# Two RMS norms ahead of matrix products, with the rows turned by a product with a diagonal of reciprocals

## The chip, the core and the metric

The kernel runs on one core of a Trainium2 chip. The core has the engines that the profile names PE (matrix products), DVE, ACT, POOL (GpSimd) and SP, which here issues the DMA transfers. The metric is the device time of one execution in microseconds, the median of several runs. Lower is better.

## The reference

A first block (attention and causal pooling, then a gated feed-forward stage with a short convolution) is followed by a second block (a state-space mixer and an mLSTM mixer side by side, then a mixture of experts). There are 256 tokens of width 1024, all in fp32. Around the change it computes:

```python
x = x + mix                                   # attention's output product
h = rmsnorm(x, norm_ffn_g)                    # first norm of this text ("ffn")
u = causal_dwconv(h @ w_up, conv_w, conv_b)
gate, val = split(u)
x = x + (silu(gate) * val) @ w_down
x = rmsnorm(x, norm_final_g)                  # end of the first block
h = rmsnorm_2(x, norm1_w)                     # second norm of this text ("n1")
p = h @ w_in_2                                # second block's input product
# rmsnorm(x, g) = x * rsqrt(mean(x*x) + EPS) * g
```

Two norms follow each other between the blocks. The kernel applies both at once. With y = x * norm_final_g, h is y * norm1_w over the root of mean(y*y) + EPS*mean(x*x) + EPS*EPS, one reciprocal per row.

## The kernel before, in words

The 256 tokens are two row tiles of 128 (t = 0, 1). X holds the residual rows, H is a scratch of the same shape. The weights come in pieces of 1 MB through a ring of five `raw` buffers. To keep fp32 accuracy, each piece is split in two fp32r parts: ACT copies it to WH (`split`, L544), DVE writes the rest raw - WH to WL (L1077). Activations are split likewise: HTH and HTL hold the transposed normed rows (feature blocks of 128 on the partitions), MXH and MXL the inputs of output and down products. `three` (L2022 to L2025) issues the three products that make one. There are three such ring slots of WH and WL. SP's queue fetches a piece when its ring buffer has been split.

Each engine runs a list written out by hand, in order, with semaphores between the engines; nothing is scheduled at run time. PE's list sets the order of the work.

The stretches of this text:

- Output product of the attention, `wo`: for t, for half c, products into bank 4 + 2c + t. Each finished bank releases DVE's `add_to_x` (L1114), which adds it into X.
- First norm. ACT squares rows of X with a row sum (`squares`, L551): all of tile 0, tile 1 in two halves. DVE makes mean + EPS (L1080, L1119), POOL raises it to -0.5 (`power`, L1973). DVE and for half of tile 1 ACT scale the rows into H (`rows` L1091, `row1` L556). PE turns H by transposes, two feature blocks per bank of 6, 7, 4, 5 (`norm_columns`, L2064). ACT writes HTH, scaled by the norm's weight (`columns`, L566), and DVE HTL (L1100). PE waits for two column blocks at a time (`col_ready`).
- `warm(n, w)` (L2029) issues n products of the identity with itself. Their result is not used. They stand in the list where PE would wait.
- Feed-forward: 11 groups g of 256 features. `feature_tiles` makes gate and value features (bank 4, 5 or 6, 7), DVE and ACT do the convolution, the silu and the split to MXH, MXL. The down product of group g - 1 follows group g's, all four quarters (t, half) into banks 0 to 3, each group's 24 products of 512 columns.
- Last group: `last_down` does tile 0 first, then tile 1's two halves.
- Second norm. DVE adds into X and writes X*g to H (`weighted_rows`, L1321). ACT squares both X and H. DVE joins the sums (L1334, L1342, L1119), scales H by the reciprocal (L1091), ACT does half of tile 1 (L556), then PE, ACT and DVE turn it as above. The first piece of the second block (`xbc`) follows.

## Time and profile before

| | us |
|---|---|
| median of three runs | 1025.98 (1025.85 to 1026.82) |
| the profiled execution | 1027.49 |
| its span, first to last instruction | 1025.70 |
| mean granted clock of PE | 0.997 |
| PE busy | 1006.3 |
| DVE busy | 840.8 |
| ACT busy | 704.4 |

The page gives each engine's busy time, and the chain of work that ended last, followed back from the end. A timeline lists one engine's instructions by start. A matmul's duration is longer than its step, since matmuls overlap: the distance from one start to the next is what it costs. An fp32 product counts as two MATMUL instructions ("x2"), an fp32 transpose as one. In brackets stands how long the engine had stood idle before and what released it.

### The profile page before, as it was taken

To read this page: it belongs to the slowest core of one execution; us is meant where nothing else is said; L and a number is where in the kernel's file an instruction comes from. 1 tells how busy PE (TensorE), PEld (TensorE's weight loads), DVE (VectorE), ACT (ScalarE), POOL (GpSimd) and SP (SyncE) were. 2 spreads that over 40 slices of the span, in tenths; PEclk is the share of its full clock that TensorE was granted. 3 is DMA by queue.
4 is the path that set the end of the run, shared out by engine and by line. 5 is a ranking of instruction groups with operands and counts; after the bars stand their busy time and mean duration, and the time that the engine had idled before them with its cause. 6 is when DMAs were issued, how large, how long until landed. Compare 5 with 4: busy or idle time off the path is not lost.

```text
span 1025.7 us, 14943 instructions
## 1 busy us (share of the span) xinstructions
PE 1006.3 (98%) x5588; PEld 869.2 (85%) x5588; DVE 840.8 (82%) x1038; ACT 704.4 (69%) x856; POOL 40.7 (4%) x44
## 2 busy tenths in 40 slices
PE   7999999999999999999999999999999999999997
PEld 6788999999989888999888888888888888888884
DVE  5855876666677887797859899999999999999987
ACT  5664655555565755576445788888888888888874
POOL 2001000000000020100220100000000000000000
PEclk9999999999999999999999999999999999999999
DMA  9734456474725455343216999999999999999971
GB/s 342 282 123 144 155 174 222 147 226 147 228 72 197 164 165 158 126 140 118 83 34 222 349 362 368 363 378 368 374 360 378 359 376 368 376 355 383 364 294 44
DMA packets 82709, 253.60 MB, mean 247 GB/s; under 512 B 4160, under 2 KB 42176, under 8 KB 62656
## 3 DMA queue, kind: packets, MB, share of 16 engines
q1 hardware_dynamic: 82624, 252.51, 68.2%
q8 instruction: 48, 0.79, 0.3%
q14 instruction: 37, 0.30, 0.1%
HBM read 251.44 MB, written 1.05 MB: 246 GB/s over the span
## 4 chain that ended last, share of the span: by engine, by line
PE 83%; DVE 7%; ACT 3%; issue 3%; POOL 0%; POOLq 0%; DVEq 0%; ACTq 0%
PE bank L2023 25%; PE bank L2025 25%; PE bank L2024 24%; DVE WL L1077 2%; ACT WH L544 2%; PE bank L2525 1%; PE bank L2565 1%; DVE CV L1369 1%; PE bank L2029 1%; PE bank L2484 0%; PE bank L2493 0%; PE bank L2597 0%; PE bank L2050 0%; PE bank L2458 0%; PE bank L2129 0%
## 5 line engine op out<-in xcount | busy, mean ns | idle before, releaser
L1077 DVE TENSOR_TENSOR WL<-raw,WH 128x2048 fp32r<-128x2048 f32 x230 | 524.6, 2303 | 89.6 <-ACT WH L544 86.0
L544 ACT ACTIVATE WH<-raw 128x2048 fp32r<-128x2048 f32 x231 | 440.6, 1914 | 82.2 <-PE bank L2025 72.2
L2023 PE MATMUL bank<-WH,MXH 128*128 128x512 f32 x552 | 218.4, 396 | 0.6 <-DVE WL L1077 0.6
L2025 PE MATMUL bank<-WH,MXL 128*128 128x512 f32 x552 | 215.2, 390 | 0.0
L2024 PE MATMUL bank<-WL,MXH 128*128 128x512 f32 x552 | 215.0, 390 | 0.0
L2023 PE MATMUL bank<-HTH,WH 128*128 128x256 f32 x576 | 165.0, 286 | 1.2 <-DVE HTL L1100 1.2
L2025 PE MATMUL bank<-HTH,WL 128*128 128x256 f32 x576 | 162.9, 283 | 0.0
L2024 PE MATMUL bank<-HTL,WH 128*128 128x256 f32 x576 | 162.9, 283 | 0.0
L2023 PE MATMUL bank<-WH,HTH 128*128 128x512 f32 x400 | 159.5, 399 | 2.3 <-DVE WL L1124 1.9
L2024 PE MATMUL bank<-WL,HTH 128*128 128x512 f32 x400 | 155.9, 390 | 0.0
L2023 PEld LDWEIGHTS bank<-WH,MXH 128*128 128x128 f32 x552 | 103.6, 188 | 29.3 <-issue 8.4
L2025 PEld LDWEIGHTS bank<-WH,MXL 128*128 128x128 f32 x552 | 103.6, 188 | 22.2
L2024 PEld LDWEIGHTS bank<-WL,MXH 128*128 128x128 f32 x552 | 103.7, 188 | 20.3
L2023 PEld LDWEIGHTS bank<-HTH,WH 128*128 128x128 f32 x576 | 110.4, 192 | 2.1 <-issue 1.5
L2024 PEld LDWEIGHTS bank<-HTL,WH 128*128 128x128 f32 x576 | 110.5, 192 | 0.5
L2025 PEld LDWEIGHTS bank<-HTH,WL 128*128 128x128 f32 x576 | 110.4, 192 | 0.0
L2023 PEld LDWEIGHTS bank<-WH,HTH 128*128 128x128 f32 x400 | 75.5, 189 | 17.8 <-issue 2.1
L2024 PEld LDWEIGHTS bank<-WL,HTH 128*128 128x128 f32 x400 | 75.3, 188 | 14.4
L2025 PE MATMUL bank<-WH,HTH 128*128 128x512 f32 x208 | 81.4, 392 | 0.0
L2025 PE MATMUL bank<-WH,HTL 128*128 128x512 f32 x200 | 78.1, 391 | 0.0
L1973 POOL TENSOR_TENSOR sm<-sm,cn 128x1 f32<-128x1 f32 (+3 forms) x18 | 17.1, 957 | 856.1 <-DVE sm L1080 509.2
L1369 DVE SCALAR_TENSOR_TENSOR CV<-bank,pt,CV 128x255 f32<-128x255 f32 (+2 forms) x84 | 40.3, 481 | 9.0 <-ACT CV L733 6.8
(411 smaller groups left out, 1063.3 us busy)
## 6 DMA issues: line engine op xcount, KB each, us to landing
raw<-in_exp_w_up SPq DMA_DIRECT2D x52, 1024.0 KB, 7.2
raw<-in_exp_w_gate SPq DMA_DIRECT2D x52, 1024.0 KB, 7.2
raw<-in_exp_w_down SPq DMA_DIRECT2D x52, 1024.0 KB, 7.4
raw<-in_w_in SPq DMA_DIRECT2D x34, 1024.0 KB, 5.2
raw<-in_w_up SPq DMA_DIRECT2D x22, 1024.0 KB, 5.3
raw<-in_w_down SPq DMA_DIRECT2D x11, 1024.0 KB, 5.2
raw<-in_w_out SPq DMA_DIRECT2D x8, 1024.0 KB, 5.1
raw<-in_w_o SPq DMA_DIRECT2D x4, 1024.0 KB, 5.4
```

The lines of the kernel that those rows point to most:

```text
L544: e.activation(WH[i % HL][:, :], raw[i % RAW][:, :], ACT.Copy).then_inc(a_wh, 1)
L1077: e.tensor_tensor(l, r, h.bitcast(F32), ALU.subtract).then_inc(v_wl, 1)
L1369: m = e.scalar_tensor_tensor(out=u[:, sh:256], in0=b[:, 0:256 - sh], scalar=ptcol(cw, n * tap + j), in1=u[:, sh:256], op0=ALU.mult, op1=AL ...
L1973: e.tensor_tensor(v, v, const("mh", v.shape[1]), ALU.pow).then_inc(g_rstd, 1)
L2023: e.matmul(out_, ah, bh, start=start, stop=False, skip_group_check=skip)
L2024: e.matmul(out_, ah, bl, start=False, stop=False, skip_group_check=skip)
L2025: return e.matmul(out_, al, bh, start=False, stop=stop, skip_group_check=skip)
L2029: e.matmul(bank[w][:, 0:128], ident, ident, start=True, stop=True)
L2525: m = e.transpose(bank[TBK][:, k * 128:(k + 1) * 128], SG[u % 2][:, k:512:4], ident)
L2565: m = e.matmul(bank[GU[0][0]][:, :], XST[kh][:, k, 0:128], raw[i % RAW][:, k * 512:(k + 1) * 512], start=(kh == 0 and k == 0), stop=(kh == ...
```

## The change

- At both norms, H is no longer written. DVE multiplies the identity by the row's reciprocals, a 128x128 diagonal (`diagonal`, into the scratch TMP), and PE multiplies X's feature blocks as stationary tile with it. That turns and scales in one. These are plain fp32 products where transposes were.
- Each feature block gets its own bank (`NORM_BANKS`), with a semaphore count for each block on PE, ACT and DVE (`bank_columns`), where there were two to a bank.
- The final norm's weight is no longer multiplied into the rows. DVE folds it into the next norm's column weight (128x8), ACT squares the weight once in the third feed-forward group (`gb2`), and the weighted square sum is a DVE instruction (`weighted_sum`) over ACT's squares of X times `gb2`.
- The last two groups' down products change order. Filler products become fewer at both places. One small weight gets another buffer.

What DVE has in its list at the second norm, from tile 0's adds on: each row is an instruction with its output, inputs and shape; x2 are two of them. Before:

```order
L1114 TENSOR_TENSOR X<-bank,X 128x512 x2
L1321 TENSOR_TENSOR H<-X,BIG 128x1024
L1114 TENSOR_TENSOR X<-bank,X 128x512
L1321 TENSOR_TENSOR H<-X,BIG 128x512
L1334 TENSOR_SCALAR sm<-sm 128x1
L1119 SCALAR_TENSOR_TENSOR sm<-sm 128x1
L1114 TENSOR_TENSOR X<-bank,X 128x512
L1321 TENSOR_TENSOR H<-X,BIG 128x512
L1342 TENSOR_SCALAR sm<-sm 128x1
L1119 SCALAR_TENSOR_TENSOR sm<-sm 128x1
L1091 TENSOR_SCALAR H<-H,sm 128x1024
L1119 SCALAR_TENSOR_TENSOR sm<-sm 128x1 x2
```

Now, from the same adds on. ISA is the weighted sum with its read-out:

```order
L1123 TENSOR_TENSOR X<-bank,X 128x512 x2
L1333 ISA CV,sm<-CV,BIG 128x512
L1333 ISA sm 128x1
L1333 ISA CV,sm<-CV,BIG,sm 128x512
L1333 ISA sm 128x1
L1123 TENSOR_TENSOR X<-bank,X 128x512
L1338 SCALAR_TENSOR_TENSOR sm<-sm 128x1
L1355 SCALAR_TENSOR_TENSOR sm<-sm 128x1
L1333 ISA CV,sm<-CV,BIG 128x512
L1333 ISA sm 128x1
L1338 SCALAR_TENSOR_TENSOR sm<-sm 128x1
L1123 TENSOR_TENSOR X<-bank,X 128x512
```

The rows X*g and their scaling (H) are gone; the last add comes behind three of the four weighted sums.

PE's list at the end of the last down product, before:

```order
L2025 MATMUL bank<-WH,MXL 128x512
L2023 MATMUL bank<-WH,MXH 128x512
L2024 MATMUL bank<-WL,MXH 128x512
L2025 MATMUL bank<-WH,MXL 128x512
L2029 MATMUL bank<-cn 128x128 x21
L2064 MATMUL bank<-cn,H 128x128 x8
L2029 MATMUL bank<-cn 128x128 x3
L2064 MATMUL bank<-cn,H 128x128 x8
L2029 MATMUL bank<-cn 128x128 x3
L2023 MATMUL bank<-HTH,WH 128x256
```

And now, where cn is the identity and TMP the diagonal:

```order
L2042 MATMUL bank<-WH,MXL 128x512
L2040 MATMUL bank<-WH,MXH 128x512
L2041 MATMUL bank<-WL,MXH 128x512
L2042 MATMUL bank<-WH,MXL 128x512
L2046 MATMUL bank<-cn 128x128 x3
L2078 MATMUL bank<-TMP,X 128x128 x8
L2046 MATMUL bank<-cn 128x128 x4
L2078 MATMUL bank<-TMP,X 128x128 x8
L2040 MATMUL bank<-HTH,WH 128x256
```

The filler of 21 products ahead of the turns is 3 now, and the turns have become products with the diagonal.

The diff, cut to its core:

```diff
+PARTS = [(0, 0, 512), (0, 512, 1024), (1, 0, 512), (1, 512, 1024)]
+NORM_BANKS = {"ffn": (6, 4, 5, 0, 1, 2, 3, 7), "n1": (6, 4, 5, 0, 1, 2, 7, 3)}
...
+        gb, gb2 = big(9216, D), big(10240, D)
+        diag = [TMP[:, t, 0:128] for t in range(T)]
-        ws_raw = big(10240, 256)
+        ws_raw = big(0, 256)
...
+                for k, w in enumerate(NORM_BANKS[name]):
+                    e.wait_ge(p_cols, COL[name, k])
+                    e.activation(dh[:, k, :], bank[w][:, 0:256], ACT.Copy, scale=ptcol(gname, k)).then_inc(a_colh, 1)
...
-            row1("ffn", X)
-            columns("ffn", "norm_ffn_g", 0, (6, 7, 4, 5), HTH)
...
+            bank_columns("ffn", "norm_ffn_g", HTH)
...
+                if g == 2:
+                    e.wait_ge(d_gb, 16)
+                    e.activation(gb2, gb, ACT.Square).then_inc(a_gb2, 1)
...
-            e.wait_ge(v_xadd, 6)
-            squares("n1", 0, X[:, 0, :], ss[:, 0:1])
-            e.wait_ge(v_fx, 1)
-            squares("n1", 1, H[:, 0, :], part[0])
-            for c in range(2):
-                cs = slice(c * 512, (c + 1) * 512)
-                e.wait_ge(v_xadd, 7 + c)
-                squares("n1", 2 + 2 * c, X[:, 1, cs], part[1 + 2 * c])
-                e.wait_ge(v_fx, 2 + c)
-                squares("n1", 3 + 2 * c, H[:, 1, cs], part[2 + 2 * c])
-            row1("n1", H)
-            columns("n1", "norm1_w_2", 0, (6, 7, 4, 5), HTH)
+            for i, (t, c0, c1) in enumerate(PARTS):
+                e.wait_ge(v_xadd, XADD["n1", i])
+                if t:
+                    e.wait_ge(v_gsum, 1 if c0 == 0 else 2)
+                e.activation(cvf[:, c0:c1], X[:, t, c0:c1], ACT.Square, accum_out=part[i]).then_inc(a_sq, 1)
+            bank_columns("n1", "norm_final_g", HTH)
...
+            def diagonal(name, t):
                 e.wait_ge(g_rstd, RSTD[name, t])
-                e.tensor_scalar(H[:, t, 0:n], src[:, t, 0:n], rs[:, t:t + 1], None, ALU.mult).then_inc(v_h0, 1)
+                e.tensor_scalar(diag[t], ident, rs[:, t:t + 1], None, ALU.mult).then_inc(v_diag, 1)
...
             mean_eps(rs[:, 0:1], ss[:, 0:1], D).then_inc(v_ms, 1)
-            e.wait_ge(a_sq, SQ["ffn", 1])
-            mean_eps(part[1], ss[:, 1:2], D).then_inc(own.up(), 1)
+            e.wait_ge(a_sq, SQ["ffn", 2])
+            mean_eps(part[4], part[0], D).then_inc(own.up(), 1)
+            diagonal("ffn", 0)
             e.wait_ge(p_used, PI["wo", 1, 1] + 1)
-            add_to_x(1, 1, 7)
-            rows("ffn", 0, X)
-            e.wait_ge(a_sq, SQ["ffn", 2])
-            chained(rs[:, 1:2], part[0], 1.0 / D, part[1]).then_inc(v_ms, 1)
-            rows("ffn", 1, X)
-            columns("ffn", "norm_ffn_g", 0, (6, 7, 4, 5), HTH, HTL)
+            add_to_x(3, 7)
+            e.wait_ge(a_sq, SQ["ffn", 3])
+            chained(rs[:, 1:2], part[1], 1.0 / D, part[4]).then_inc(v_ms, 1)
+            diagonal("ffn", 1)
+            bank_columns("ffn", "norm_ffn_g", HTH, HTL)
...
-            def weighted_rows(t, c0, c1):
-                e.tensor_tensor(H[:, t, c0:c1], X[:, t, c0:c1], gb[:, c0:c1], ALU.mult).then_inc(v_fx, 1)
+            def weighted_sum(i, start):
+                t, c0, c1 = PARTS[i]
+                e.wait_ge(a_sq, SQ["n1", i])
+                e.wait_ge(own.sem, own.n)
+                return e.tensor_tensor_reduce(cvf[:, c0:c1], cvf[:, c0:c1], gb2[:, c0:c1], 1.0 / D, start, ALU.mult, ALU.add,
+                                              wsum[:, i:i + 1])
+            def eps_of(i, start):
+                e.wait_ge(own.sem, own.n)
+                e.scalar_tensor_tensor(out=esum[:, i:i + 1], in0=part[i], scalar=EPS / D, in1=start, op0=ALU.mult,
+                                       op1=ALU.add).then_inc(own.up(), 1)
+            ng = ptcol("norm_final_g", 0, 8)
+            e.tensor_tensor(ng, ng, ptcol("norm1_w_2", 0, 8), ALU.mult).then_inc(own.up(), 1)
             e.wait_ge(p_tok0, TOK0["fin0"])
-            add_to_x(0, 0, 0)
-            add_to_x(0, 1, 1)
-            e.wait_ge(d_gb, 16)
-            e.wait_ge(v_xadd, 6)
-            weighted_rows(0, 0, D)
+            add_to_x(0, 0)
+            add_to_x(1, 1)
+            e.wait_ge(a_gb2, 1)
+            weighted_sum(0, EPS * EPS).then_inc(v_gsum, 1)
+            e.wait_ge(v_gsum, 1)
+            weighted_sum(1, wsum[:, 0:1]).then_inc(v_gsum, 1)
             e.wait_ge(p_tok0, TOK0["fin1"])
-            add_to_x(1, 0, 2)
-            e.wait_ge(v_xadd, 7)
-            weighted_rows(1, 0, 512)
-            e.wait_ge(a_sq, SQ["n1", 0])
-            e.tensor_scalar(part[5], ss[:, 0:1], EPS / D, EPS * EPS, ALU.mult, ALU.add).then_inc(own.up(), 1)
-            e.wait_ge(a_sq, SQ["n1", 1])
-            chained(rs[:, 0:1], part[0], 1.0 / D, part[5]).then_inc(v_ms, 1)
+            add_to_x(2, 2)
+            e.wait_ge(v_gsum, 2)
+            eps_of(0, wsum[:, 1:2])
+            e.wait_ge(own.sem, own.n)
+            e.scalar_tensor_tensor(out=rs[:, 0:1], in0=part[1], scalar=EPS / D, in1=esum[:, 0:1], op0=ALU.mult,
+                                   op1=ALU.add).then_inc(v_ms, 1)
+            weighted_sum(2, EPS * EPS).then_inc(own.up(), 1)
+            eps_of(2, wsum[:, 2:3])
             e.wait_ge(p_used, PI["down", NG - 1] + 1)
-            add_to_x(1, 1, 3)
-            e.wait_ge(v_xadd, 8)
-            weighted_rows(1, 512, D)
-            e.wait_ge(a_sq, SQ["n1", 2])
-            e.tensor_scalar(part[6], part[1], EPS / D, EPS * EPS, ALU.mult, ALU.add).then_inc(own.up(), 1)
-            e.wait_ge(a_sq, SQ["n1", 3])
-            chained(part[7], part[2], 1.0 / D, part[6]).then_inc(own.up(), 1)
-            rows("n1", 0, H)
-            e.wait_ge(a_sq, SQ["n1", 4])
-            chained(part[6], part[3], EPS / D, part[7]).then_inc(own.up(), 1)
-            e.wait_ge(a_sq, SQ["n1", 5])
-            chained(rs[:, 1:2], part[4], 1.0 / D, part[6]).then_inc(v_ms, 1)
-            rows("n1", 1, H)
-            columns("n1", "norm1_w_2", 0, (6, 7, 4, 5), HTH, HTL)
+            add_to_x(3, 3)
+            diagonal("n1", 0)
+            weighted_sum(3, esum[:, 2:3]).then_inc(own.up(), 1)
+            e.wait_ge(own.sem, own.n)
+            e.scalar_tensor_tensor(out=rs[:, 1:2], in0=part[3], scalar=EPS / D, in1=wsum[:, 3:4], op0=ALU.mult,
+                                   op1=ALU.add).then_inc(v_ms, 1)
+            diagonal("n1", 1)
+            bank_columns("n1", "norm_final_g", HTH, HTL)
...
+            def norm_columns(name, t):
+                e.wait_ge(v_diag, DIAG[name, t])
+                for k, w in enumerate(NORM_BANKS[name]):
+                    if t == 0 and name == "ffn" and k == 7:
+                        e.wait_ge(v_xadd, XADD["ffn", 3])
+                    m = e.matmul(bank[w][:, t * 128:(t + 1) * 128], X[:, t, k * 128:(k + 1) * 128], diag[t], start=True,
+                                 stop=True)
                     if t:
                         m.then_inc(p_cols, 1)
...
-                if cols and k % 2 == 0:
+                if cols in NORM_BANKS:
+                    e.wait_ge(v_coll, COL[cols, k])
+                elif cols and k % 2 == 0:
                     e.wait_ge(v_coll, COL[cols, k // 2])
...
-            warm(5, 0)
-            norm_columns("ffn", 0, (6, 7, 4, 5))
-            warm(2, 0)
-            norm_columns("ffn", 1, (6, 7, 4, 5))
-            warm(3, 0)
...
+            wo_half(0, 0, 0, 512).then_inc(p_tok0, 1)
+            wo_half(0, 1, 0, 512).then_inc(p_tok0, 1)
+            wo_half(1, 0, 0, 512).then_inc(p_used, 1)
+            wo_half(1, 1, 0, 512).then_inc(p_used, 1)
+            norm_columns("ffn", 0)
+            warm(1, 0, 256)
+            norm_columns("ffn", 1)
...
+            def last_down(g, f, t, c0, n):
+                j, s = 2 * g + f, 2 * (g % 2) + f
+                wh, wl = last_w[g - NG + 2]
+                ts, hf, cs = slice(t * 128, (t + 1) * 128), c0 // 512, slice(c0, c0 + n)
+                return three(bank[2 * t + hf][:, c0 % 512:c0 % 512 + n], MXH[:, s, ts], MXL[:, s, ts], wh[:, f, cs],
+                             wl[:, f, cs], False, j == FF - 1)
+            last_w.append(piece(PI["down", NG - 2], 2))
+            e.wait_ge(v_mxl, FF - 2)
+            for c0 in (0, 512):
+                for f in range(2):
+                    last_down(NG - 2, f, 0, c0, 512)
+            for f in range(2):
+                last_down(NG - 2, f, 1, 0, 512)
+            last_w.append(piece(PI["down", NG - 1], 2))
             for f in range(2):
                 e.wait_ge(v_mxl, FF - 1 + f)
-                for hf in range(2):
-                    m = last_down(0, hf, f)
+                for c0 in (0, 512):
+                    m = last_down(NG - 1, f, 0, c0, 512)
             m.then_inc(p_tok0, 1)
-            for hf in range(2):
-                for f in range(2):
-                    m = last_down(1, hf, f)
-                m.then_inc(p_used if hf else p_tok0, 1)
-            warm(21, 7)
-            norm_columns("n1", 0, (6, 7, 4, 5))
-            warm(3, 0)
-            norm_columns("n1", 1, (6, 7, 4, 5))
-            warm(3, 0)
+            for f in range(2):
+                m = last_down(NG - 2, f, 1, 512, 512)
+            m.then_inc(p_used, 1)
+            for f in range(2):
+                m = last_down(NG - 1, f, 1, 0, 512)
+            m.then_inc(p_tok0, 1)
+            for f in range(2):
+                m = last_down(NG - 1, f, 1, 512, 512)
+            m.then_inc(p_used, 1)
+            warm(3, 7)
+            norm_columns("n1", 0)
+            warm(4, 7, 256)
+            norm_columns("n1", 1)
...
```

## Rows read from the trace of the kernel before

**Rows 1.** The page, its chain that ended last, shares of the span by engine.
```profile
PE 83%; DVE 7%; ACT 3%; issue 3%; POOL 0%; POOLq 0%; DVEq 0%; ACTq 0%
```

**Rows 2.** Timeline of PE, first norm: start, duration, line, operation [idle before <-releaser].
```profile
98.41 1.27 PE L2029 MATMUL bank<-cn 128*128 128x128 f32 x10
...
101.46 1.09 PE L2064 MATMUL bank<-cn,H 128*128 128x128 f32 x8
...
103.83 0.35 PE L2023 MATMUL bank<-HTH,WH 128*128 128x256 f32 x1 [0.61 <-DVE HTL L1100]
```

**Rows 3.** Timeline of PE, second norm and the piece behind it.
```profile
290.80 4.85 PE L2029 MATMUL bank<-cn 128*128 128x128 f32 x42
...
297.72 1.09 PE L2064 MATMUL bank<-cn,H 128*128 128x128 f32 x8
...
300.09 0.35 PE L2023 MATMUL bank<-HTH,WH 128*128 128x256 f32 x1 [0.61 <-DVE HTL L1100]
...
306.05 0.28 PE L2023 MATMUL bank<-HTH,WH 128*128 128x256 f32 x1
```

**Rows 4.** Timeline of DVE and ACT over the same stretch.
```profile
98.61 0.69 DVE L1114 TENSOR_TENSOR X<-bank,X 128x512 f32<-128x512 f32 x1 [1.08 <-PE bank L2025]
...
99.34 0.63 ACT L551 ACTIVATE CV<-X 128x512 f32<-128x512 f32 x1 [2.00 <-DVE X L1114]
...
100.09 0.16 DVE L1119 SCALAR_TENSOR_TENSOR sm<-sm 128x1 f32<-128x1 f32 x1
100.92 0.49 DVE L1091 TENSOR_SCALAR H<-X,sm 128x512 f32<-128x512 f32 x1 [0.67 <-POOL sm L1973]
...
101.94 3.02 ACT L566 ACTIVATE HTH<-bank,pt 128x256 fp32r<-128x256 f32 x8 [0.30 <-PE bank L2064]
102.81 3.23 DVE L1100 SCALAR_TENSOR_TENSOR HTL<-bank,pt,HTH 128x256 fp32r<-128x256 f32 x8 [1.40 <-ACT HTH L566]
104.80 3.76 ACT L544 ACTIVATE WH<-raw 128x2048 fp32r<-128x2048 f32 x2
106.80 4.49 DVE L1077 TENSOR_TENSOR WL<-raw,WH 128x2048 fp32r<-128x2048 f32 x2 [0.76 <-ACT WH L544]
```

**Rows 5.** Timeline of PE, the gate piece: second feature tile, next piece.
```profile
106.91 0.28 PE L2023 MATMUL bank<-HTH,WH 128*128 128x256 f32 x1
...
109.79 0.28 PE L2023 MATMUL bank<-HTH,WH 128*128 128x256 f32 x1
```

**Rows 6.** Timeline of PE, attention: plain fp32 products.
```profile
46.79 0.44 PE L2128 MATMUL bank<-BIG,H 128*128 128x128 f32 x2
...
61.31 0.39 PE L2154 MATMUL bank<-BIG 128*128 128x128 f32 x2
61.53 0.39 PE L2155 MATMUL bank<-BIG 128*128 128x128 f32 x2
```

**Rows 7.** Timeline of DVE ahead of the second norm.
```profile
285.26 0.42 DVE L1315 TENSOR_TENSOR MXL<-CV,MXH 128x256 fp32r<-128x256 f32 x1 [0.55 <-ACT MXH L706]
287.06 2.29 DVE L1077 TENSOR_TENSOR WL<-raw,WH 128x2048 fp32r<-128x2048 f32 x1 [1.38 <-ACT WH L544]
289.27 1.28 DVE L1114 TENSOR_TENSOR X<-bank,X 128x512 f32<-128x512 f32 x2
```

**Rows 8.** DVE groups by form: line, operation, count | busy us, mean ns | idle.
```profile
L1829 DVE SCALAR_TENSOR_TENSOR CV<-bank,sm,CV 128x512 f32<-128x512 f32 x26 | 19.4, 747 | 1.0 <-PE bank L2025 1.0
...
L1514 DVE CUSTOM_DVE_ANT_0 BIG<-bank,BIG 128x256 f32<-128x256 f32 x8 | 3.4, 419 | 0.0
```

**Rows 9.** Waits of ACT from 98 to 285: us in total, times, longest.
```profile
ACT WH L544 <- PE bank L2025: 25.4, 10, 2.8
```

**Rows 10.** PE timeline, and a window (us, busy of 5 engines, PEclk, DMA).
```profile
12.54 0.47 PE L2023 MATMUL bank<-WH,HTH 128*128 128x512 f32 x1 [1.90 <-DVE WL L1124]
...
535.47 3.04 PE L2458 MATMUL bank<-BIG 128*128 128x36 f32 x24
...
538.00:541.00 3.00, 3.00 (x15) 3.00 (x15) 2.21 (x16) 0.21 (x1) 0.00 (x0) 0.50 0.00 0
```

More of the change, by code:

```diff
@@ L113 @@
 COL = numbered([(s, j) for s in ("mix", "attn", "ffn", "n1", "ssd0", "ssd1", "ml0", "ml1")
-                for j in range(4 if s in ("mix", "ffn", "n1") else 2)])
+                for j in range({"mix": 4, "ffn": 8, "n1": 8}.get(s, 2))])
 P_CUM = numbered(["sums", "turned", "max"])
@@ L119 @@
                 + ["ssd0", "ssd1", "ml0", "ml1"] + [(s, t) for s in ("n2", "out") for t in range(T)])
-SQ = numbered([("mix", t) for t in range(T)] + [("ffn", i) for i in range(3)] + [("n1", i) for i in range(6)]
+PARTS = [(0, 0, 512), (0, 512, 1024), (1, 0, 512), (1, 512, 1024)]
+XADD = numbered([(n, i) for n in ("ffn", "n1") for i in range(4)] + [("out", i) for i in range(4)])
+SQ = numbered([("mix", t) for t in range(T)] + [("ffn", i) for i in range(1, 4)] + [("n1", i) for i in range(4)]
               + [("n2", c, t) for c in range(2) for t in range(T)] + [("out", i) for i in range(3)])
@@ L1104, in columns, with bank_columns @@
                     m.then_inc(v_coll, 1)
+            def bank_columns(name, gname, dh, dl):
+                for k, w in enumerate(NORM_BANKS[name]):
+                    e.wait_ge(a_colh, COL[name, k])
+                    e.scalar_tensor_tensor(out=dl[:, k, :], in0=bank[w][:, 0:256], scalar=ptcol(gname, k),
+                                           in1=dh[:, k, :].bitcast(F32), op0=ALU.mult,
+                                           op1=ALU.subtract).then_inc(v_coll, 1)
             def evac(name, t, piece):
@@ L1355, in vector @@
[L1355 removed]
+            mean_eps(part[5], part[0], D).then_inc(own.up(), 1)
+            chained(r1[:, 0:1], part[1], 1.0 / D, part[5]).then_inc(v_ms, 1)
+            mean_eps(part[6], part[2], D).then_inc(own.up(), 1)
+            chained(r1[:, 1:2], part[3], 1.0 / D, part[6]).then_inc(v_ms, 1)
             def residual(t):
@@ L2025, in three, with warm @@
                 return e.matmul(out_, al, bh, start=False, stop=stop, skip_group_check=skip)
-            def warm(n, w):
+            def warm(n, w, c=0):
                 for _ in range(n):
-                    e.matmul(bank[w][:, 0:128], ident, ident, start=True, stop=True)
+                    e.matmul(bank[w][:, c:c + 128], ident, ident, start=True, stop=True)
             def piece(i, k):
```

100 lines of the change are left out of this document (40 added, 60 removed).

## The prediction

> **What bounds the kernel now.** I read the page first: the chain that ended last is 83% PE [rows 1]. So a change counts only where PE stands still or does work that is thrown away. The granted clock was full over nearly the whole span. Then I read the timeline of PE at the two norms the diff touches; there the reader should look for the `ident` products of `warm` (L2029), which compute nothing and only fill waits. After the attention's output product PE starts filler at 98.41, turns two row tiles, and starts the first useful product at 103.83 [rows 2]. That is 5.42 us. After the last down product filler starts at 290.80 and useful work at 300.09, 9.29 us [rows 3]. Together 14.7 us, 1.4% of the time, is all that the two norms can give. Third, the timelines of DVE and ACT over the same stretches, for what sets these starts.
>
> At the first norm it is a chain on tile 1: last add to X at 98.61, square at 99.34, scalar step at 100.09, the power on GpSimd, row scaling at 100.92 (0.49 us for half a row), PE's turn at 101.46, ACT's HTH columns at 101.94, DVE's HTL columns at 102.81 and PE at 103.83 [rows 2, 4]. From then on PE takes a column block whenever DVE has it. The gate's second feature tile starts at 106.91, the next piece at 109.79 [rows 5].
>
> **First norm, what changes.** Everything up to 100.92 stays: same adds, squares and power. Then:
> - DVE scales a 128x128 diagonal instead of 512 columns. The 512 took 0.49 us and a one-column step 0.16 [rows 4]; I take 0.24. PE starts at 101.21 instead of 101.46 (bounds 101.13 and 101.46).
> - PE makes plain products, two passes each, instead of one-pass turns. The nearest rows are fp32 products 128x128 with a new stationary tile each time: pairs start 0.22 us apart at 61.31 and 61.53, and the two passes take 0.39. After a switch of kind, at 46.79, they took 0.44 [rows 6]. I take 0.224 per product, at worst 0.28. Eight take 1.8 us, so PE has tile 1 done at 103.0. Tile 0's eight lie in the time that filler had.
> - ACT starts after the first product rather than after two turns. The delay is the same two passes, 0.48 us (101.46 to 101.94 [rows 2, 4]), so ACT starts at 101.69.
> - DVE waited for two ACT columns and now waits for one. Eight ACT columns take 3.02, eight of DVE 3.23 [rows 4]: a step is 0.37 on ACT and 0.39 on DVE. So DVE starts 0.5 after ACT, at 102.19 rather than 102.81. It ends at 105.42 instead of 106.04.
> - PE may take each block as it is ready, not each pair. After the last block 3 products are left instead of 6, 0.36 us less. PE's own work ends at the same point (103.0 plus 24 products of 0.12, from the 2.88 us between 106.91 and 109.79). The second feature tile starts at about 105.95, 0.96 earlier.
> - What is late next is the split of the following weight piece. ACT starts it 2.86 us after its first column (104.80 after 101.94), so at 104.55 and DVE's half at 106.55 rather than 106.80; it takes 2.29, so PE can start at about 109.0. PE itself would be there at 108.83. Gain: 109.79 less 108.98, **0.81 us**. Bounds: 0.3 with products of 0.28 and the diagonal at 0.49; 1.0 if the split is no limit.
>
> **Last down product and second norm.** The order of the products changes so that tile 0 is done after 30 of 48 rather than 24. Two effects. PE now comes to the last MXL block at about 285.33, and that block is only ready at 285.68 (285.26 plus 0.42 [rows 7]), so PE waits half a microsecond and ends at 291.3 instead of 290.8. This costs nothing as long as DVE is the later one: DVE is in a split until 289.35 (287.06 plus 2.29), and its adds start at 289.27 in the kernel before [rows 7]. For the same reason the earlier tile 0 earns nothing. If that cover went, the price is 0.5.
>
> DVE's chain decides. New are four weighted sums of squares, one behind each add's square. The nearest row is the same custom instruction on 256 elements, 0.42 us (one source in PSUM); scaled by its neighbours I take 0.70 for 512. Upper bound 0.83: the 512 three-source form at 0.75 [rows 8] plus a read-out. Lower bound 0.6, the step between two 512 adds [rows 7]. Gone are the product rows X*g and their squares on ACT. With 0.69 per add and 0.75 from a square's start to the step that reads it (99.34 to 100.09 [rows 4]):
> - adds at 289.33 and 289.93, first weighted sum 290.8 to 291.5, second to 292.3;
> - add of tile 1's first half 292.2, its square until 293.7, third weighted sum to 294.4, last add at 294.58;
> - tile 0's diagonal ends at 295.43, PE starts its products at 295.5 (tile 0 has slack);
> - from the last add to the second diagonal: the first norm took 2.31 us from add to scaling (98.61 to 100.92 [rows 4]), plus 0.78 for the fourth weighted sum and its wait. That is 297.67; PE starts tile 1 at 297.97. Before it was 297.72 [rows 3].
>
> So the start is 0.25 **later**, and the finer hand-over gives it back. PE's eight products end at 299.76, then 24 products: second feature tile at 302.7, where it now is 303.17 (306.05 less 2.88). ACT's columns start at 298.45, the split of the next piece 2.86 later as above, at 301.31 (now 297.72 + 0.48 + 2.86 = 301.06), and PE can start that piece at 305.74 rather than 306.05. Gain: **0.31 us**. Bounds: a loss of 0.5 (weighted sums 4 x 0.13 dearer, products at 0.28) and a gain of 1.2 (the waits in front of the four sums, about 0.9 in my list, vanish).
>
> **Edits priced at nothing.** The 1024-element square of the weight on ACT in the third FFN group, about 1.1 us: ACT waits for PE ten times there, 25.4 us in all [rows 9]. If it hit PE it would cost its 1.1. The 128x8 product of two weights is one short DVE step. The wider weight table and the moved buffer for the small projection's weights change no order on the DMA queue. Two more one-column steps behind the split are beside PE's work.
>
> **Sum.** 0.81 + 0.31 = 1.12 us. The profiled execution took 1027.49 (span 1025.70, 1.79 outside it) and would take 1026.37. The median of the timed runs is 1.51 lower, 1025.98; the sum carried over is 1024.86. A shift at these places moves all that follows: PE is the chain's engine up to the end, and the experts' weights are fetched only after the routing, which shifts too.
>
> **Rivals.**
> - *The clock drops in the wait (slower).* PE had 42 passes of filler, 4.85 us, ahead of the second norm [rows 3]; now it has 3 products, ends them at 292.0 and idles until 295.5. Before, this trace has one dip of the granted clock: in the routing, from 538 to 541, it was 0.50, the level of 1.2 GHz [rows 10], and what came ahead were products of only 36 columns. Against it: near 12.5 PE had stood still for 1.9 us [rows 10], and the products behind that came at full pace. Nothing here is as long as 3.5. If it drops, 3.0 us at 0.50 cost 1.5 us of work, its two edges a little more; I take 1.7. Then 1024.86 + 1.7 = 1026.6, slower than before. It decides from the point where half-rate work reaches tile 1's products; a second dip in a row gives 1028.3.
>  The Trainium skill, "TensorE: Matmul & The Clock Gate", section "HAM oscillation — how this bites in real kernels", says that long idle gaps between bursts return PE to half rate and that each restart is then paid cold; by it this rival would be the rule and the time 1026.6. The same page, "Part 4: PE-mode transpose", says that transposes don't count as busy for that gate; by it the new plain products would help to hold the clock and the forecast would stand. No row here separates the two.
> - *The weighted sums and the two-pass products are dearer.* Both at their upper bounds: 0.3 at the first norm, minus 0.4 at the second. 1026.0; half way it is 1025.5. For it: four of them lie in line on one engine. Against: each row of a similar form sits near my value.
> - *More comes back.* The waits ahead of the sums vanish and the split is no limit: 1.0 + 1.2 gives 1023.8. Against it: each sum needs a square that can start only after the add before it.
> - *The gain is taken back later*, by DVE or by weight transfers in the experts' stage: 1026.0.
>
> **How the numbers follow.** Forecast 0.50 (own range 1024.2 to 1025.7); clock 0.22, of which 0.06 with two dips; dearer steps 0.13; more comes back 0.11; taken back 0.04. 0.2% is 2.05 us, about what a measurement of this kernel can tell from no change, so the bounds are 1023.93 and 1028.03. Faster: most of the fourth case and a little of the forecast's tail, 0.15. Slower: two dips and a little of one, 0.09. The rest, 0.76, is within. The range leaves out the far end of "more comes back" and two dips: 1023.6 to 1027.2.
>
> **What would show it.** First norm: the first HTH-by-WH product about 4.6 us after the last output product instead of 5.4, products 0.22 apart, and the next piece 10.6 us after it instead of 11.4. Second norm: PE idle for about 3.5 us, tile 1's first product 3.4 us after the last add's start, the granted clock at 1.00. The forecast is wrong if the clock row for that stretch shows 0.5, if PE waits for MXL and DVE is no longer the later one, or if a weighted sum takes over 0.85 us.

## The result: a little slower, and why the profiled runs hide it

| | before | after |
|---|---|---|
| median, runs | 1027.15 us, 17 | 1028.24 us, 17 |
| ratio after to before, 95% | | 1.0016 [1.0009, 1.0024] |
| profiled execution, span | 1027.49, 1025.7 | 1027.69, 1025.8 |

The forecast was 1.1 us faster; measured is about 1.6 us slower (0.0016 x 1026; the means of the 17 runs differ by 1.6 too, their medians by 1.1). That is within 0.2%, but outside the range given: carried over to the 1025.98 that the forecast starts from, it is 1027.6, and the range ended at 1027.2. The two profiled spans are equal by chance. The kernel before had a fall of the clock in its routing [rows 10], and after had none there, which is 0.9 us. The remaining 0.7 us come in the experts' stage: at 600 us after is 0.75 us behind, at the last product 0.1. That stage scatters from one trace to the next (e15, described below, goes from 1.1 us ahead to 0.5 behind in it). So I compare starts of the same PE instruction in both traces, ahead of these stages, and not spans.

At the first norm, PE's timeline after (start, duration, line) answers to [rows 2, 5]:

```profile
98.47 1.95 PE L2078 MATMUL bank<-TMP,X 128*128 128x128 f32 x16
...
101.32 2.05 PE L2078 MATMUL bank<-TMP,X 128*128 128x128 f32 x16 [0.68 <-DVE TMP L1092]
103.13 0.36 PE L2040 MATMUL bank<-HTH,WH 128*128 128x256 f32 x1
...
109.06 0.39 PE L2040 MATMUL bank<-HTH,WH 128*128 128x256 f32 x1
```

The x16 are eight products of two passes each. From the end of the output products (98.47 after, 98.41 before) to the next piece it is 10.59 us (109.06 less 98.47); before it was 11.38 (109.79 less 98.41). The gain is 0.79.

At the second norm, it answers to [rows 3]:

```profile
290.69 0.83 PE L2046 MATMUL bank<-cn 128*128 128x128 f32 x6
294.94 3.68 PE L2078 MATMUL bank<-TMP,X 128*128 128x128 f32 x16 [3.42 <-DVE TMP L1092]
298.44 1.07 PE L2046 MATMUL bank<-cn 128*128 128x128 f32 x8
299.35 1.95 PE L2078 MATMUL bank<-TMP,X 128*128 128x128 f32 x16
301.06 0.36 PE L2040 MATMUL bank<-HTH,WH 128*128 128x256 f32 x1
```

Same stretch, windows (us, busy time of PE, PEld, DVE, ACT, POOL, then the granted clock, as in [rows 10]):

```profile
292.00:294.00 2.00, 0.00 (x0) 0.00 (x0) 1.40 (x6) 0.72 (x2) 0.54 (x1) 1.00 0.90 306
294.00:295.00 1.00, 0.06 (x1) 0.06 (x1) 0.88 (x3) 0.28 (x1) 0.00 (x0) 1.00 0.00 0
295.00:298.00 3.00, 3.00 (x14) 3.00 (x15) 1.21 (x4) 0.45 (x2) 0.55 (x1) 0.51 0.00 0
298.00:299.00 1.00, 1.00 (x9) 1.00 (x8) 0.00 (x0) 0.00 (x0) 0.00 (x0) 0.77 0.00 0
299.00:302.00 3.00, 3.00 (x29) 3.00 (x28) 1.72 (x5) 2.23 (x7) 0.00 (x0) 1.00 0.00 0
```

PE stood still for 3.42 us; then the granted clock fell to 0.5, the 1.2 GHz level. Tile 0's products took 3.68 us where the first norm's took 1.95. Tile 1's could not start before 299.35, though its diagonal was written by 297.38, as DVE's timeline shows:

```profile
294.00 0.68 DVE L1123 TENSOR_TENSOR X<-bank,X 128x512 f32<-128x512 f32 x1
294.60 0.28 DVE L1092 TENSOR_SCALAR TMP<-cn,sm 128x128 f32<-128x128 f32 x1
295.48 0.75 DVE L1333 CUSTOM_DVE_ANT_0 CV<-CV,BIG,sm 128x512 f32<-128x512 f32 x1 [0.59 <-ACT CV L722]
...
297.09 0.29 DVE L1092 TENSOR_SCALAR TMP<-cn,sm 128x128 f32<-128x128 f32 x1 [0.66 <-POOL sm L1990]
```

A second loss lies 38 us further on. At the small projection's turn (`small_turn`, the transpose of a narrow tile) PE waits for ACT's copy of a bank. First the two rows of the kernel before, of a stretch the prediction did not look at (ACT, then PE), then PE's of after. ACT, before:

```profile
337.25 0.36 ACT L778 ACTIVATE TMP<-bank 32x256 f32<-32x256 f32 x1
```

PE, before:

```profile
337.66 0.31 PE L2279 MATMUL bank<-cn,TMP 32*128 32x32 f32 x2
```

PE, after:

```profile
339.44 0.31 PE L2312 MATMUL bank<-cn,TMP 32*128 32x32 f32 x2 [0.68 <-ACT TMP L780]
```

Before, ACT's copy ended at 337.61 (337.25 + 0.36) and PE took it at 337.66, without a wait: two chains arrived together, and either could have been the later. After, PE waits. What comes ahead of ACT's copy is VectorE's convolution, whose first taps are, before and after:

```profile
305.61 1.50 DVE L1369 SCALAR_TENSOR_TENSOR CV<-bank,pt,CV 128x255 f32<-128x255 f32 x3
```

```profile
307.39 1.50 DVE L1386 SCALAR_TENSOR_TENSOR CV<-bank,pt,CV 128x255 f32<-128x255 f32 x3
```

In both kernels ACT's copy starts 31.64 us behind the first tap (337.25 and 339.03). The taps are 1.78 us later in after, and so is the turn.

### The profile page after: what moved, and what is told of

It reads as the page before. It is cut to its first block, busy times and chain, and to the rows that moved or that the text cites. A ratio compares the mean times of both kernels' runs of the same rounds, so it can differ in the third digit from the quotient of the medians.

```text
span 1025.8 us, 14887 instructions
## 1 busy us (share of the span) xinstructions
PE 1003.7 (98%) x5562; PEld 867.6 (85%) x5562; DVE 839.5 (82%) x1043; ACT 701.9 (68%) x851; POOL 40.8 (4%) x44
## 4 chain that ended last, share of the span: by engine, by line
PE 81%; DVE 9%; ACT 5%; issue 2%; POOL 0%; POOLq 0%; DVEq 0%; ACTq 0%
PE bank L2040 24%; PE bank L2042 24%; PE bank L2041 24%; DVE WL L1079 4%; ACT WH L549 3%; DVE CV L1386 1%; PE bank L2558 1%; PE bank L2598 1%; PE bank L2078 1%; PE bank L2517 0%; PE bank L2526 0%; PE bank L2067 0%; PE bank L2145 0%; PE bank L2491 0%; PE bank L2630 0%
```

## The experiments

All twelve were timed in five rounds beside the kernel before. The table has the ratio to the kernel before, what it is in us (of 1026), and how much later than before the same PE instruction starts in the profiled execution, at four points, named by their time in the trace of before. The first useful product is the first HTH-by-WH product behind the second norm; "next piece" is, as in the prediction, the product that begins with the following piece of weights. From each I took off the shift at 12.54 us, which is start-up noise (-0.16 to 0.90 us).

| kernel | ratio [95%] | us | 109.79 next piece | 300.09 first useful product | 337.66 small turn | 471.51 |
|---|---|---|---|---|---|---|
| after | 1.0016 [1.0009, 1.0024] | +1.6 | -0.71 | +0.99 | +1.80 | +1.68 |
| e1_fill18 | 1.0005 [0.9996, 1.0015] | +0.5 | -0.72 | -0.67 | +0.15 | +0.03 |
| e3_fill_turns | 1.0002 [0.9993, 1.0011] | +0.2 | -0.71 | -0.65 | +0.15 | +0.03 |
| e4_before_fill3 | 1.0012 [1.0003, 1.0021] | +1.2 | 0.00 | +0.81 | +0.82 | +0.83 |
| e5_first_norm | 0.9992 [0.9983, 1.0001] | -0.8 | -0.79 | -0.91 | -0.90 | -0.91 |
| e6_old_order | 1.0006 [0.9997, 1.0015] | +0.6 | -0.73 | -0.67 | +0.13 | +0.01 |
| e9_split_early | 0.9989 [0.9980, 0.9998] | -1.1 | -0.73 | -0.67 | -0.79 | -1.15 |
| e10_before_delay | 1.0008 [0.9999, 1.0017] | +0.8 | 0.00 | +0.01 | +0.63 | +0.59 |
| e11_all | 0.9988 [0.9979, 0.9997] | -1.2 | -0.70 | -0.65 | -0.76 | -1.20 |
| e12_both_early | 0.9986 [0.9977, 0.9995] | -1.4 | -0.82 | -0.87 | -0.98 | -1.43 |
| e13_pairs | 1.0003 [0.9995, 1.0012] | +0.3 | +0.11 | +0.90 | +0.90 | +0.45 |
| e14_early_no_fill | 1.0002 [0.9994, 1.0011] | +0.2 | -0.72 | +0.95 | +0.84 | +0.46 |
| e15_first_early | 0.9991 [0.9982, 1.0000] | -0.9 | -0.89 | -1.12 | -1.11 | -1.11 |

The last column and the timed difference agree within 0.6 us in each row, though each interval is about 1 us to either side. So the steps are read from the traces, one for each kernel, and the timings say no more than that their sum lasts to the end. I stop at 471.51 because the routing behind it sometimes has a fall of the clock of its own, and the experts' stage scatters.

Each timed run also has a mean granted clock. Its median is 0.996 to 0.997 in the three kernels that leave PE idle for over 3 us at the second norm (after, e4, e14), and 0.998 or 0.999 in the other ten and in the runs of the kernel before beside them. One fall of 3.4 us to half would lower the mean by 0.0017 (an estimate, 3.4 x 0.5 of 1026). So the fall at the norm is there in most runs, not only in the profiled ones.

**e1_fill18: the wait filled.**

```diff
-            warm(3, 7)
+            warm(18, 7)
             norm_columns("n1", 0)
```

> The changed kernel with 18 filler products in place of 3 ahead of the second norm's first tile; nothing else differs. Clock theory (PE stands idle for 3.4 us there, and the granted clock falls from 1.00 to 0.50 for the next 3 us): PE idle ahead of the tile falls from 3.42 us to under 0.2, the granted clock is 1.00 from 290 to 300, the 16 products of the first tile take 1.95 us as at the first norm and not 3.68, the next piece (the first product after the second norm, at 306.99 in the changed kernel) starts 1.9 us earlier, and the run is 1.6 to 2.0 us below the changed kernel and about 1 below the kernel before. Rival (the new chain of weighted sums and the fp32 products with a diagonal are what costs): the products stay near 3.7 us or the chain's end moves by nothing, and the time is the changed kernel's within 0.3.

PE's timeline:

```profile
291.03 4.18 PE L2046 MATMUL bank<-cn 128*128 128x128 f32 x36
295.25 2.05 PE L2078 MATMUL bank<-TMP,X 128*128 128x128 f32 x16
297.14 1.06 PE L2046 MATMUL bank<-cn 128*128 128x128 f32 x8
298.03 1.95 PE L2078 MATMUL bank<-TMP,X 128*128 128x128 f32 x16
299.74 0.36 PE L2040 MATMUL bank<-HTH,WH 128*128 128x256 f32 x1
```

and its window:

```profile
295.00:298.00 3.00, 2.96 (x26) 2.77 (x26) 1.40 (x5) 0.72 (x2) 0.55 (x1) 1.00 0.00 0
```

The clock held and the products took 2.05 us. The first useful product and the next piece came 1.66 us earlier than in after (0.99 + 0.67 in the table); 1.9 was expected for the next piece. The time fell by about 1.1 us rather than 1.6 to 2.0, and it did not get below the kernel before: the wait of 0.68 us at the small turn stayed. That sent me to the second loss.

**e3_fill_turns: other filler.** As e1, but 3 products and 30 turns:

```diff
             warm(3, 7)
+            for _ in range(30):
+                e.transpose(bank[7][:, 0:128], ident, ident)
             norm_columns("n1", 0)
```

> The changed kernel with 3 filler products and then 30 turns of 128 x 128 with the identity ahead of the second norm's first tile, some 3.3 us of work in the place of the idle 3.4 us. If any work of PE holds the clock: as the kernel with 18 filler products, 1.00 from 290 to 300, 1.6 to 2.0 us below the changed kernel. If turns do not count as work for the clock (the Trainium skill, TensorE: Matmul & The Clock Gate, on PE-mode transposes): 0.50 behind them, products of 3.7 us, and the changed kernel's time within 0.3.

PE's timeline:

```profile
291.56 3.44 PE L2298 MATMUL bank<-cn 128*128 128x128 f32 x30
295.10 2.05 PE L2078 MATMUL bank<-TMP,X 128*128 128x128 f32 x16
```

3.44 us of turns kept the clock as well as products did. The rule of the Trainium skill ("TensorE: Matmul & The Clock Gate", "Part 4: PE-mode transpose") that transposes don't count as busy is not borne out here, for fp32 turns of this shape and over this length. It rests on one trace and on the mean clock of the 11 runs, 0.998 to 0.999.

**e4_before_fill3: the old kernel with the wait left empty.**

```diff
-            warm(21, 7)
+            warm(3, 7)
```

> The kernel before with 3 filler products in place of 21 ahead of its second norm, so that PE idles there for about 4.2 us; nothing else differs. Clock theory: the granted clock falls to 0.50 behind the idle time, the turns and filler of that norm run at half speed, and the time rises by 0.7 to 2.0 us. Rival (idle time alone is harmless, the fall belongs to the new products or their chain): clock 1.00, and the time of the kernel before within 0.3.

PE's timeline, and below it a window with the granted clock:

```profile
296.08 1.35 PE L2064 MATMUL bank<-cn,H 128*128 128x128 f32 x8 [4.29 <-DVE H L1091]
297.22 1.49 PE L2029 MATMUL bank<-cn 128*128 128x128 f32 x6
298.50 1.87 PE L2064 MATMUL bank<-cn,H 128*128 128x128 f32 x8
```

```profile
297.00:300.00 3.00, 3.00 (x16) 3.00 (x16) 0.49 (x1) 1.55 (x4) 0.30 (x1) 0.50 0.00 0
```

The idle time alone brings the fall, with the old chain and the old turns. It costs 0.8 us there and 1.6 in the changed kernel. That fits with half as much work ahead of the first useful product, sixteen one-pass turns against sixteen two-pass products, but no run separates this from the later start of the fall in e4 (0.7 us behind PE's first turn, against 0.1 behind the first product in after). With e1 and the mean clocks this shows the fall and what brings it. It does not show how long the idle time must be: waits of 1.3 to 2.2 us at 12.54 were followed by products at full pace in every trace that has one, waits of 3.38 us and more at the norm by 0.50, and nothing in between was run.

**e5_first_norm.** The kernel before with the change at the first norm alone. The core of the edit, with the same diagonal and bank-by-bank columns as in the change:

```diff
-            norm_columns("ffn", 0, (6, 7, 4, 5))
...
-            norm_columns("ffn", 1, (6, 7, 4, 5))
...
+            bank_norm(0)
+            warm(1, 0, 256)
+            bank_norm(1)
```

> The kernel before with the change at the first norm alone (products with a diagonal, a bank per block of columns); its second norm, last down and final norm are the old ones. If the first norm's gain of 0.79 us seen in the trace lasts to the end: 0.6 to 0.9 us below the kernel before. If it is given back at a later wait (for data or in the routing): within 0.3 of it.

-0.8 timed, -0.79 at the next piece and -0.91 at 471.51. The first norm's gain lasts. (It was 0.69 at 262 us and 0.91 at 300, so 0.22 of it appeared over the old second norm; where it comes from is open.)

**e6_old_order.** e1 with the old order of the last down product (the two whole groups in sequence, in the last one tile 0 then tile 1).

```diff
-            for c0 in (0, 512):
-                for f in range(2):
-                    last_down(NG - 2, f, 0, c0, 512)
...
+            def last_down(t, hf, f):
```

> The kernel with 18 filler products, with the old order of the last down product put back (whole pairs of groups, tile 0 done after 24 of 48 products in place of 30). In the changed kernel the stage enters the last down product 0.63 us earlier than before and leaves it only 0.11 earlier, after a wait of 0.22 us for the last MXL block. Order theory: with the old order the wait goes, the last down product ends 0.4 to 0.55 us earlier (about 290.2 to 290.6), but the diagonals come at most 0.1 earlier, since VectorE's adds, which stand behind a weight split, set them; the time is that of the kernel with 18 filler products within 0.3. Rival (the end of the product sets the norm): the next piece and the time come 0.5 us earlier.

The filler begins at 290.21 rather than 291.03, of which 0.28 is the start-up shift, so the last down product ends 0.54 us earlier. But the diagonals and the first useful product do not move: -0.67 in both. As forecast, the new order costs 0.5 us while VectorE is the later one, and earns nothing.

**e9_split_early: the second chain.** e1 with ScalarE's split of the next piece ahead of its columns:

```diff
+            split(PI["xbc", 0] + 1)
             bank_columns("n1", "norm_final_g", HTH)
-            split(PI["xbc", 0] + 1)
```

> The kernel with 18 filler products, with ScalarE's half of the split of the next weight piece put ahead of its eight columns of the second norm; nothing else differs. With 18 filler products PE starts its first useful product 0.35 us earlier than the kernel before, yet 38 us later, at its small turn (L2312 <- ACT TMP), it waits 0.7 us and is 0.47 us later than before. Theory: from the second norm to that turn the chain of VectorE and ScalarE (split, then taps of the convolution) sets the time, not PE; with ScalarE's split out of the way VectorE's starts 0.8 to 1.1 us earlier, the wait at the small turn falls under 0.1, and the run is 0.7 to 0.8 us below the kernel with 18 filler products. Rival (the wait at the small turn has another source, the small weights' buffer that was moved, say): the wait stays at 0.7 and the time is the same.

PE's row at the small turn, with no wait:

```profile
336.71 0.31 PE L2312 MATMUL bank<-cn,TMP 32*128 32x32 f32 x2
```

DVE, where its split no longer waits for ACT:

```profile
298.49 3.23 DVE L1110 SCALAR_TENSOR_TENSOR HTL<-bank,pt,HTH 128x256 fp32r<-128x256 f32 x8 [1.27 <-ACT HTH L573]
301.63 2.28 DVE L1079 TENSOR_TENSOR WL<-raw,WH 128x2048 fp32r<-128x2048 f32 x1
```

The small turn comes 0.94 us earlier than in e1, and the product at 471.51 by 1.18; timed, 1.6. That is more than the 0.7 to 0.8 expected. The part between the small turn and 471.51 I did not trace. The split costs nothing in its new place: ACT did nothing there in after between 295.45 and 299.77.

**e10_before_delay: the same chain in the old kernel.**

```diff
             split(PI["xbc", 0] + 1)
+            e.tensor_scalar(H[:, 0, :], H[:, 0, :], 1.0, None, ALU.mult).then_inc(own.up(), 1)
             mean_eps(r1[:, 0:1], ss[:, 0:1], D).then_inc(v_ms, 1)
```

> The kernel before with one more VectorE operation of 1024 columns (about 1 us, it rewrites a buffer that is free) between the split behind the second norm and the first taps; nothing else differs. If VectorE's chain sets the time up to the small turn and had almost no slack in the kernel before: PE waits 0.8 to 1.0 us at the small turn (L2279 <- ACT TMP) and the time rises by as much. If PE sets it and VectorE had room: no wait there and the kernel before's time within 0.2.

DVE with the added step, and below it PE at the small turn:

```profile
305.22 0.69 DVE L1353 TENSOR_SCALAR H<-H 128x1024 f32<-128x1024 f32 x1
305.82 0.21 DVE L1080 TENSOR_SCALAR sm<-sm 128x1 f32<-128x1 f32 x2
```

```profile
338.23 0.31 PE L2280 MATMUL bank<-cn,TMP 32*128 32x32 f32 x2 [0.56 <-ACT TMP L778]
```

The step was 0.60 us long (305.22 to 305.82), not 1, and PE waited 0.56 us for it. So the kernel before had 0.04 us of room at this point. A later VectorE was paid here almost in full.

**e11_all.** Filler, old order, early split, and VectorE's four one-column steps behind the convolution:

```diff
                 conv(c, (4, 5) if c % 2 else (6, 7))
 
+            fin_sums()
```

> The changed kernel with all that the traces so far point to mended: 18 filler products, the old order of the last down product, ScalarE's split ahead of its columns, and VectorE's four one-column steps for the final norm (0.54 us) put behind the convolution. Theory: clock at 1.00 at the norm, no wait at the small turn, PE's next piece after the second norm 0.3 to 0.8 us earlier than in the kernel with 18 filler products; time 1.0 to 1.5 us below that kernel and 0.8 to 1.5 below the kernel before. Rival (the gain is handed to another wait behind the small turn): the same as the kernel with the split alone put early.

The same as e9 at every point within 0.05 us: once the split is early, the two other edits give nothing, which is what the rival said. The size expected, 0.8 to 1.5 below the kernel before, was met (1.2), but the next piece came only 0.07 us earlier than in e1, not 0.3 to 0.8.

**e14_early_no_fill.** After with the early split alone.

> The changed kernel with ScalarE's split of the next piece put ahead of its columns and nothing else: 3 filler products as in the changed kernel. It gives the price of the clock alone, with the wait at the small turn out of the way. Theory: PE idle 3.4 us, granted clock 0.50 for about 3.4 us behind it, first tile's products 3.7 us, no wait at the small turn; first useful product and small turn 1.3 to 1.8 us later than with 18 filler products and the early split, time 1.2 to 1.8 us above that kernel's 1025.9 (1027.1 to 1027.7). Rival (the slow clock is hidden behind the waits for VectorE's chain): within 0.4 of 1025.9.

PE's timeline, and below it the window behind the idle time:

```profile
295.83 3.50 PE L2078 MATMUL bank<-TMP,X 128*128 128x128 f32 x16 [3.38 <-DVE TMP L1092]
```

```profile
296.00:299.00 3.00, 3.00 (x16) 3.00 (x17) 1.20 (x4) 2.13 (x3) 0.54 (x1) 0.53 0.00 0
```

The clock's price alone: 1.62 us at the first useful product against e9 (0.95 + 0.67), and 1.61 at 471.51. The timed medians are 1.15 us apart, the ratios 1.3.

**e13_pairs.** e11 with `k | 1` in place of `k` in the three waits of the hand-over.

```diff
-                    e.wait_ge(v_coll, COL[cols, k])
+                    e.wait_ge(v_coll, COL[cols, k | 1])
```

> The kernel with all four mends, but at both norms every block waits for its neighbour too (p_cols, a_colh and v_coll for k | 1), so that blocks go from PE to ScalarE to VectorE to PE in pairs as in the kernel before. If the hand-over block by block is what gives the gain: the first useful product comes 0.6 to 0.9 us later at both norms, the next piece 0.3 to 0.5 later at the first one, and the time is 0.4 to 1.0 above the kernel with all mends. If the split behind the columns sets the next piece in any case: the next piece and the time within 0.2.

Block by block is worth more than I expected: 0.81 us at the first norm's next piece (+0.11 against -0.70) and as much again at the second, 1.65 together at 471.51; timed, 1.5 against 0.4 to 1.0 expected. With pairs nothing is left of the gain at the first norm. PE does not wait for the split at the next piece when columns come in pairs.

**e12_both_early.** e11 with the same move at the first norm (`split(13)` ahead of `bank_columns("ffn", ...)`).

> The kernel with all four mends and, at the first norm too, ScalarE's split of the next piece ahead of its columns. ScalarE stands idle for 1.73 us there before its columns in the changed kernel and the split takes 1.9, so the columns start 0.1 to 0.3 us later, but PE's wait of 0.4 us for the split piece goes. Expected: next piece 0.0 to 0.3 us earlier, time equal to the kernel with all mends within 0.3. Rival (the weight slot comes free late, and ScalarE is held up): columns over 0.5 us later and the time 0.3 or more above.

DVE's timeline there, which answers to its row at 106.80 in [rows 4]:

```profile
105.50 4.48 DVE L1079 TENSOR_TENSOR WL<-raw,WH 128x2048 fp32r<-128x2048 f32 x2
```

ACT's columns still start at 101.85, the next piece comes 0.12 us earlier and the second one behind it too (0.23 at 471.51 against e11). This is the fastest kernel here, 0.9986 [0.9977, 0.9995]; its lead on e9 and e11 is seen in the trace only.

**e15_first_early.** e5 with that move. It tells what the second norm's part is worth once mended.

> The kernel before with the change at the first norm alone and, there, ScalarE's split of the next piece ahead of its columns; second norm, last down and final norm are the old ones. Beside the kernel with all mends at both norms it tells what the second norm's part of the change is worth once it is mended. If that part earns what the traces show (small turn of the fully mended kernel at 336.9 against 337.7 before, of which 0.65 came from the first norm): 0.1 to 0.6 us above the fully mended kernel's 1025.35. If it earns nothing: within 0.1 of it. Both norms: next piece at about 109.0.

At 471.51 it is 0.32 us behind e12; timed 0.9991 against 0.9986, too close to call. So nearly all the good of the change is in its first half. Over the second norm itself the old form is even ahead: e15's first useful product comes 0.25 us before e12's (-1.12 against -0.87) and its next piece 0.14 (-1.12 against -0.98). What e12 has at 471.51 it gains behind the small turn, and that I did not trace. Part of e12's lag is filler that is now too long. DVE and PE of e12, ahead of tile 1's products:

```profile
296.89 0.29 DVE L1092 TENSOR_SCALAR TMP<-cn,sm 128x128 f32<-128x128 f32 x1 [0.66 <-POOL sm L1989]
```

```profile
296.62 1.06 PE L2045 MATMUL bank<-cn 128*128 128x128 f32 x8
297.52 1.95 PE L2077 MATMUL bank<-TMP,X 128*128 128x128 f32 x16
```

The diagonal is written by 297.18, and PE comes out of its four filler products only at 297.52. At the first norm PE started 0.05 us behind the diagonal. About 0.3 us could be had here by one or two products less (an estimate from these rows; no run has it).

## Why the prediction was wrong, step by step

- **First norm, -0.81: right.** -0.79. The products were 0.224 us apart, as taken from [rows 6]: eight took 1.81 us from the first start to the first useful product (101.32 to 103.13). The hand-over by single blocks is all of the gain: with pairs the next piece is 0.11 us later than before (e13).
- **Last down order, priced at nothing: right.** The wait for MXL was 0.22 us rather than 0.5, though the order costs 0.54 in all. Tile 0's earlier end earned nothing (e6).
- **VectorE's chain: right.** From the last add to the second diagonal I had 3.09 us, and it was 3.09 (294.00 to 297.09). The weighted sums took 0.69 and 0.75 for 0.70.
- **The clock: the step that failed.** I had seen PE's idle time (3.5 us, measured 3.42) and priced the fall at 1.7 (measured 1.6), but gave it a chance of 0.22. The argument against was that 1.90 us of idle time at 12.54 had done no harm [rows 10]; that row says nothing of 3.4. The sentence on the Trainium skill's "HAM oscillation — how this bites in real kernels" (long idle gaps return PE to half rate) pointed to the right case, and the trace agrees, with 0.51 from 295 to 298. The kernel before spent 42 passes of filler in this place [rows 3]. I read them as work thrown away; e4 shows that they bought 0.8 us. This alone is 1.6 of the 2.7 us between forecast and result. And the trace of before had rows on long idle times, at its two ends. I wrote that it has one fall of the clock; it has a second behind PE's last product (timeline of PE, then windows as above):

```profile
1019.05 0.39 PE L2598 MATMUL bank<-WL,HTL 128*128 128x512 f32 x1
```

```profile
1019.00:1022.00 3.00, 0.44 (x2) 0.01 (x1) 2.13 (x6) 0.88 (x3) 0.55 (x1) 1.00 0.46 180
1022.00:1023.00 1.00, 0.00 (x0) 0.00 (x0) 0.27 (x1) 0.56 (x1) 0.00 (x0) 0.75 0.00 0
1023.00:1024.00 1.00, 0.00 (x0) 0.00 (x0) 0.00 (x0) 0.00 (x0) 0.00 (x0) 0.50 0.56 211
```

  PE was done at 1019.44, and the clock was at 0.50 from about 1022.5; it costs nothing there, as PE has no work left. At the start PE waits 4.78 us for its input, and then:

```profile
4.78 3.65 PE L2050 MATMUL bank<-cn,X 128*128 128x128 f32 x16 [4.78 <-DMA X<-in_x]
8.22 2.42 PE L2029 MATMUL bank<-cn 128*128 128x128 f32 x18
```

  These sixteen turns are 0.22 us apart (4.78 to 8.22) and 417 ns long. Turns of the same shape at 80.7 us are 270 ns long, and eight of them take 1.09 us at the norms [rows 2, 3]. The clock column says 1.00 here, but the pace is that of the slow stretches (e4's eight turns at 0.50 took 1.87 us). Neither place is a wait between two stretches of work, yet both speak for the rival, and it deserved more than 0.22.
- **"The gain carries to the end": the step whose failure I did not see.** I wrote that PE is the chain's engine up to the end, that the new one-column steps lie beside PE's work, and gave a gain taken back later 0.04, looking for it at the experts. It was taken back at the small turn: 0.81 us (from +0.99 at the first useful product to +1.80, and 0.80 to 0.82 in e1, e3 and e6). The chain's shares [rows 1] average over the whole span and don't show how close a second chain is. In this stretch two chains ran level, within 0.04 us (e10). ScalarE's split of the next piece came 1.58 us later (the rows below) where PE's first useful product came 0.97 later, because the finer hand-over makes PE earlier against the end of the columns, and not ScalarE; and four one-column steps in place of three added 0.2. The rest of the convolution follows VectorE. That ScalarE's split is the cause is shown by e9, and that there was no room by e10. ACT's split in before and in after:

```profile
301.06 1.96 ACT L544 ACTIVATE WH<-raw 128x2048 fp32r<-128x2048 f32 x1
```

```profile
302.64 1.96 ACT L549 ACTIVATE WH<-raw 128x2048 fp32r<-128x2048 f32 x1
```

- **Second norm, -0.31: too high.** With the clock held and the split early, the next piece gains 0.16 us from 262 us on (e12: -0.82 at 262, -0.98 at 306); with the split late, 0.08 (e1). Even that is not the new norm's own: behind the changed first norm the old second one gains 0.23 over the same stretch (e15: -0.89 at 262, -1.12 at 306).

So with the right clock term alone the sum would still have been 1026.6, and the result carried over is 1027.6; the small turn and the second norm are the rest. The sum as it came out, from the trace of after: -0.71 (first norm), +0.10 (up to 262), +1.60 (262 to 300, the second norm with its clock), +0.81 (small turn), -0.12 (up to 471): +1.68, where the runs say +1.6.

## What to carry to other kernels

Filler ahead of a wait is part of the clock's upkeep: before cutting it, ask how long PE will then stand still, and look for rows with an idle time of that length, at the two ends of the trace too. If there is none, the fall is an open question and not a remote chance. Fit the filler to the wait as well: too much of it delays the work behind it. A step that makes PE start earlier may only have moved the point where it meets another engine's chain: look for the next place where PE takes something from that chain, and for how close the two rows stand there. When two engines end level, first look for an operation that can be moved into idle time ahead of them; here one moved line was worth 1.2 us in the traces and 1.6 timed, more than the whole forecast.

## What the runs showed that I had not expected

- Profiled executions had a fall of the clock at this norm (after, e4, e14) or in the routing (before, e4, e15). Each time it lasted 3.4 us, whatever work followed. At the norm it came behind 3.38 to 4.29 us of idle PE, and in the routing while PE was busy with narrow products; why it comes there, and only in some traces, is open. The norm's fall is not there in every run: two of the 17 runs of after had a mean granted clock of 1.000 and spans of 1024.4 and 1024.7 us, against a median span of 1026.4. Six had 0.995 and spans from 1027.4 to 1028.9, which fits with a second fall in the same run; no trace of such a run of after was kept.
- In the routing the fall costs the kernel before 0.9 us: the kernels without it gain that between 471.51 and 548.27 (e1, start-up shift left in: +0.34 to -0.53; after: +1.66 to +0.77).
- A VectorE multiply by a scalar, 1024 columns of fp32 in SBUF, took 0.69 us, and 0.60 to the next step. I had assumed about 1 from the 0.49 for 512 columns [rows 4].
